# Input pieces and the order of the first tiles in a two-layer decoder kernel

## The chip, the cores and the metric

The kernel runs on one core of a Trainium2 chip. The time is the device time of one execution in microseconds (us), lower is better. Times of a kernel are compared as medians of several runs, and a profiler took one execution of the kernel before apart.

## The reference

A trunk of two layers runs over 512 prompt tokens and 8 decode tokens of width 1024, everything in float32. Each layer is two half-weighted feed-forward blocks around a mixer, each followed by a layer norm:

```
x <- LN(alpha*x + 0.5*SwiGLU_1(x))        D_MODEL = 1024, D_FF = 2816
x <- LN(alpha*x + mixer(x))               mixer: sparse attention (layer 0), pooling (layer 1)
x <- LN(alpha*x + 0.5*SwiGLU_2(x))
def _swiglu(x, w_i, w_o):
    h = jnp.einsum('btd,df->btf', x, w_i)
    gate, up = h[..., :D_FF], h[..., D_FF:]
    return jnp.einsum('btf,fd->btd', jax.nn.silu(gate) * up, w_o)
```

What matters here is the very first block: its input `x_prompt` (512 x 1024) and `x_sample` (8 x 1024), and its weights `ffn1_wi`.

## The kernel before

**Layout.** The activations live transposed in SBUF: `xf[p, d, t]` holds feature `128*d + p` of token `t`, for 8 tiles d of 128 features and 520 tokens. For precision each float32 matrix product is made of three products of a reduced float32 type: a tile is split into a high part (rounded) and a low part (the rest), for `x` as `xh` and `xl`, for the weights as `w_hi` and `w_lo`. TensorE (PE) multiplies hi*hi, hi*lo and lo*hi.

**Weights.** SyncE (SP) loads weight chunks of 1 MB into two buffers `w_raw` (L418: two DMAs of 512 KB for each chunk of `ffn1_wi`, in runs of 128 numbers, 512 bytes). ScalarE (ACT) makes `w_hi` in `split_hi` (L511), VectorE (DVE) makes `w_lo` in `split_lo` (L1221). SP may load chunk c once `s_lo` has reached c+1, which starts at 2: chunks 0 and 1 are loaded at once, chunk 2 after `split_lo(0)`.

**The start.** ACT issues eight DMAs (L733 to L741): the prompt's input as one DMA of 2 MB into `x_in` (rows of 4 KB), the decode input, the table of constants `const` (its first 128 columns are the identity that a transpose on PE needs), the page table twice, and three for the layer norms' parameters. All eight count on one semaphore, `s_in`. PE waits for all of them, transposes the parameters (L1169), then for each d the 4 token tiles of the prompt (L1175) and the 8 decode tokens (L1176) into PSUM; three pairs of banks take turns, so tile d waits for the copy of tile d-3 (`s_ev`). ACT runs `split_hi(0)` and `split_hi(1)` and only then copies `xf` to `xh` (L747). DVE runs `split_lo(0)` and `split_lo(1)`, then copies the parameters (L1698, L1700) and the tiles `xf` out of PSUM (L1704, L1705). GpSimd (POOL) waits for the eight DMAs, computes two columns of indices (L1842), starts a gather of 2 MB of cached keys (`fetch_half(0)`, L1749) and then computes `xl` (L1851).

**The first products.** In `two_chunks` PE multiplies the first half of the tokens with chunk 0, then with chunk 1, then the second half with both (192 matmuls, L797). It waits for `s_ev` at 8, for `s_lo` of the chunk, and for each tile's `xh`, and before the lo*hi part for each tile's `xl`. From there the loop over the chunks runs on, each engine in the fixed order of its program, to the end of the kernel. The gathered half of keys is written on by POOL at L1755, after the first two tiles of the hidden layer.

## Time and profile before

| | |
|---|---|
| median of 3 runs | 2185.98 us (2183.97 to 2189.35) |
| the profiled execution's own time | 2186.89 us |
| its span, first to last instruction | 2185.1 us |
| PE matmul busy | 2007.9 us (92%) |
| DVE, ACT, POOL busy | 856.9, 598.6, 513.3 us |
| HBM traffic | 81 GB/s over the span |

The profiled execution's own time is 1.8 us above its span and 0.9 us above the median. Every time below counts from the start of the span.

### The profile page before, as it was taken

Reading aid. Unit: us, or ns where it says so; the run is one execution under the profiler, and the core shown is the slowest. Engines: PE = TensorE matmul, PEld = TensorE weight load, DVE = VectorE, ACT = ScalarE, POOL = GpSimd, SP = SyncE. Lnnn points to the kernel's source line nnn. Section 1 sums busy time; section 2 is a strip of 40 time slices with the busy share of each in tenths; the row PEclk is TensorE's granted clock in tenths of the full one; section 3 lists DMA queues with packets and bytes.
Section 4 is the critical chain, followed back from the end, with each engine's and each line's share of the span. In section 5 each row is a group of like instructions: output and inputs, shape, how many; then the busy total and the mean of one; then the engine's idle time right before and its main releaser. Section 6 shows DMA issues by size and latency. Waiting matters only on the chain.

```text
span 2185.1 us, 36160 instructions
## 1 busy us (share of the span) xinstructions
PE 2007.9 (92%) x15485; PEld 1912.5 (88%) x15485; DVE 856.9 (39%) x1163; ACT 598.6 (27%) x837; POOL 513.3 (23%) x438
## 2 busy tenths in 40 slices
PE   5999999999897677999999999999998379999996
PEld 5999999976885457899999989999998379999996
DVE  2433322535836622543332254333224663333223
ACT  2221221422133242522122143212123452122123
POOL 2211121331400063511112132111121751111120
PEclk9999999988959868999999999999999689999998
DMA  5453322251100032233322322333221223332321
GB/s 169 135 173 96 89 83 99 69 145 39 42 1 1 5 94 78 58 96 96 96 83 83 105 78 77 96 96 93 82 101 33 59 60 96 96 88 85 101 74 40
DMA packets 258366, 179.55 MB, mean 82 GB/s; under 512 B 10806, under 2 KB 254782, under 8 KB 257757
## 3 DMA queue, kind: packets, MB, share of 16 engines
q1 hardware_dynamic: 250000, 154.90, 24.3%
q10 hardware_dynamic: 6165, 10.79, 1.8%
q0 software_dynamic: 2112, 12.59, 1.7%
q8 instruction: 67, 1.10, 0.2%
q14 instruction: 22, 0.18, 0.0%
HBM read 169.57 MB, written 8.08 MB: 81 GB/s over the span
## 4 chain that ended last, share of the span: by engine, by line
PE 81%; issue 6%; DVE 5%; ACT 3%; POOL 3%; DMA 1%; ACTq 0%; POOLq 0%; DVEq 0%
PE ps L797 69%; PE ps L896 3%; PE ps L840 2%; PE ps L901 1%; PE ps L998 1%; PE ps L914 1%; DVE xf L1247 1%; DVE xf L1253 1%; ACT w_hi L511 1%; DVE w_lo L1221 1%; PE ps L980 1%; POOL diag L1810 1%; PE ps L881 1%; POOL sum_sq L1734 1%; ACT xf L547 1%
## 5 line engine op out<-in xcount | busy, mean ns | idle before, releaser
L797 PE MATMUL ps<-xh,w_hi 128*128 128x260 f32 x3040 | 640.0, 286 | 39.5 <-ACT xh L542 17.8
L797 PE MATMUL ps<-xh,w_lo 128*128 128x260 f32 x3040 | 633.4, 284 | 0.0
L1221 DVE TENSOR_TENSOR w_lo<-w_raw,w_hi 128x2048 fp32r<-128x2048 f32 (+2 forms) x153 | 444.9, 2909 | 408.8 <-ACT w_hi L511 408.8
L797 PEld LDWEIGHTS ps<-xh,w_hi 128*128 128x128 f32 x3040 | 486.5, 191 | 45.1 <-issue 25.9
L797 PEld LDWEIGHTS ps<-xh,w_lo 128*128 128x128 f32 x3040 | 487.6, 191 | 0.2
L797 PE MATMUL ps<-xl,w_hi 128*128 128x260 f32 x3040 | 383.9, 283 | 1.3 <-POOL xl L1838 1.3
L797 PEld LDWEIGHTS ps<-xl,w_hi 128*128 128x128 f32 x3040 | 372.8, 189 | 1.7 <-POOL xl L1838 1.7
L511 ACT CAST w_hi<-w_raw 128x2048 fp32r<-128x2048 f32 (+2 forms) x153 | 281.9, 1843 | 283.2 <-PE ps L797 262.7
L797 PE MATMUL ps<-hh,w_hi 128*128 128x260 f32 x1408 | 292.9, 283 | 0.0
L797 PE MATMUL ps<-hh,w_lo 128*128 128x260 f32 x1408 | 291.4, 282 | 0.0
L1664 DVE TENSOR_TENSOR hid<-silu_g,ps 128x520 f32<-128x520 f32 x88 | 61.3, 696 | 548.5 <-ACT silu_g L710 514.7
L710 ACT ACTIVATE silu_g<-ps 128x520 f32<-128x520 f32 x88 | 53.3, 606 | 760.4 <-PE ps L797 760.4
L1742 POOL CAST hh<-hid 128x520 f32 (+1 forms) x88 | 54.6, 620 | 789.3 <-DVE hid L1664 789.3
L797 PEld LDWEIGHTS ps<-hh,w_lo 128*128 128x128 f32 x1408 | 224.1, 188 | 0.1
L797 PEld LDWEIGHTS ps<-hh,w_hi 128*128 128x128 f32 x1408 | 223.9, 188 | 0.1
L797 PE MATMUL ps<-hl,w_hi 128*128 128x260 f32 x1408 | 177.5, 282 | 0.0
L797 PEld LDWEIGHTS ps<-hl,w_hi 128*128 128x128 f32 x1408 | 172.1, 188 | 0.0
L1744 POOL TENSOR_TENSOR hl<-hid,hh 128x520 f32 (+1 forms) x88 | 115.7, 1314 | 14.3 <-POOL hh L1742 14.1
L1732 POOL TENSOR_TENSOR sum_z<-sum_z,xf 128x520 f32<-128x520 f32 x36 | 58.3, 1619 | 200.3 <-DVE xf L1229 196.5
L1870 POOL TENSOR_TENSOR xl<-xf,xh 128x260 fp32r<-128x260 f32 x64 | 70.4, 1118 | 101.1 <-ACT xf L547 100.7
L1734 POOL TENSOR_TENSOR sum_sq<-sum_sq,silu_g 128x520 f32<-128x520 f32 x36 | 68.5, 1903 | 0.0
L519 ACT ACTIVATE silu_g<-xf 128x520 f32<-128x520 f32 x36 | 22.7, 639 | 133.6 <-DVE xf L1229 120.1
(250 smaller groups left out, 1594.3 us busy)
## 6 DMA issues: line engine op xcount, KB each, us to landing
w_raw<-in_ffn_wi_dram SPq DMA_DIRECT2D x176, 512.0 KB
w_raw<-in_ffn_wo_dram SPq DMA_DIRECT2D x32, 1024.0 KB
w_raw<-in_ffn_wo_dram SPq DMA_DIRECT2D x16, 768.0 KB
w_raw<-in_attn_w_in_dram SPq DMA_DIRECT2D x8, 1024.0 KB
keys_scratch<-key_half POOLq DMA_DIRECT2D x2, 2048.0 KB, 7.9
w_raw<-in_attn_w_o_dram SPq DMA_DIRECT2D x4, 1024.0 KB
x_in<-in_x_prompt_dram ACTq DMA_DIRECT2D x1, 2048.0 KB
out_dram<-y_out ACTq DMA_DIRECT2D x4, 512.0 KB
```

What stands on the lines that cost most here:

```text
L511: nc.scalar.copy(w_hi[:, c % 2, 0:n], w_raw[:, c % 2, 0:n]).then_inc(s_hi, 1)
L710: nc.scalar.activation(halves(silu_g[:, j % 2, :]), ps[:, 4 * (j % 2):4 * (j % 2) + 2, 0:HT], ACT.Silu).then_inc(s_silu, 1)
L797: mm = nc.tensor.matmul(ps[0:mc, bank + 2 * m + h, 0:HT], w[:, k, m, 0:mc], x(k)[:, h * HT:(h + 1) * HT], start=first and k == 0 and w is ...
L840: mm = nc.tensor.matmul(ps[:, 2 * q + h, 0:HT], mean_ones, x[:, cols(h)], start=n == 0, stop=n == 2)
L896: nc.tensor.matmul(ps[0:mc, bank + h, 0:HT], w[:, k, m, 0:mc], xh[:, k, cols(h)], start=k == 0 and w is wh, stop=False)
L1221: nc.vector.tensor_tensor(w_lo[:, c % 2, 0:n], w_raw[:, c % 2, 0:n], w_hi[:, c % 2, 0:n].bitcast(F32), ALU.subtract).then_inc(s_lo, 1)
L1664: nc.vector.tensor_tensor(halves(hid[:, j % 2, :]), halves(silu_g[:, j % 2, :]), ps[:, b + 2:b + 4, 0:HT], ALU.mult).then_inc(s_free, 2)
L1732: nc.gpsimd.tensor_tensor(sum_z[:], sum_z[:], xf[:, d, :], ALU.add).then_inc(s_sum, 1)
L1734: nc.gpsimd.tensor_tensor(sum_sq[:], sum_sq[:], sq[:, d % 2, :], ALU.add).then_inc(s_sum, 1)
L1742: nc.gpsimd.tensor_copy(hh_ij, hid[:, j:j + 1, :]).then_inc(s_hh, 1)
L1744: nc.gpsimd.tensor_tensor(hl_ij, hid[:, j:j + 1, :], hh_ij.bitcast(F32), ALU.subtract).then_inc(s_hl, 1)
L1870: nc.gpsimd.tensor_tensor(xl[:, d, cols(h)], xf[:, d, cols(h)], xh[:, d, cols(h)].bitcast(F32), ALU.subtract).then_inc(s_x, 1)
```

## The change

The identity (128 columns of the table) and the decode input are loaded first, on a semaphore of their own. The prompt's input follows as four DMAs of 256 columns each (512 KB, rows of 1 KB), each with its own semaphore; the rest of the table and the five small DMAs come behind. PE starts a pair of tiles when its piece is there, uses four pairs of banks, and transposes the parameters last, just before the first product. ACT takes `xh` of tiles 0 to 2, then `split_hi(0)`, the other five `xh`, then `split_hi(1)`. DVE copies tiles 0 to 4, runs `split_lo(0)`, copies tiles 5 to 7, then the parameters, then runs `split_lo(1)`. POOL computes all `xl` ahead of the gather.

```diff
--- before.py
+++ after.py
@@ -261,6 +261,8 @@
 
 
         s_in = sem("s_in")
+        s_const = sem("s_const")
+        s_xin = [sem(f"s_xin{n}") for n in range(4)]
         s_raw = [sem("s_raw0"), sem("s_raw1")]
         s_hi = sem("s_hi")
         s_lo = sem("s_lo")
@@ -730,21 +732,24 @@
                 tail(ffn_w[name][2], st, 4 + 2 * (st.group + KF), nxt, False, not before_pool and nxt is not None,
                      POOL_ORDER if before_pool else range(KD), before_pool)
 
-            act.dma_start(x_in[:, 0:NQT, :], a["x_prompt"][0].rearrange("(i p) d -> p i d", p=P)).then_inc(s_in, 16)
-            act.dma_start(x_in[0:DEC, NQT, :], a["x_sample"].rearrange("b t d -> (b t) d")).then_inc(s_in, 16)
-            act.dma_start(const[:], a["c_table"]).then_inc(s_in, 16)
+            act.dma_start(const[:, 0:P], a["c_table"][:, 0:P]).then_inc(s_const, 16)
+            act.dma_start(x_in[0:DEC, NQT, :], a["x_sample"].rearrange("b t d -> (b t) d")).then_inc(s_const, 16)
+            for n in range(4):
+                act.dma_start(x_in[:, 0:NQT, 256 * n:256 * n + 256],
+                              a["x_prompt"][0, :, 256 * n:256 * n + 256].rearrange("(i p) d -> p i d", p=P)).then_inc(s_xin[n], 16)
+            act.dma_start(const[:, P:CONST_COLS], a["c_table"][:, P:CONST_COLS]).then_inc(s_in, 16)
             act.dma_start(table[:], a["page_table"].rearrange("(o b) n -> o (b n)", o=1).broadcast_to([P, DEC * N_PAGES]))\
                .then_inc(s_in, 16)
             act.dma_start(page_col[:], a["page_table"].rearrange("b (n o) -> (b n) o", o=1)).then_inc(s_in, 16)
             act.dma_start(lnp_rows[0:48, :], a["ln_g"].rearrange("l n (d p) -> (l n d) p", p=P)).then_inc(s_in, 16)
             act.dma_start(lnp_rows[48:96, :], a["ln_b"].rearrange("l n (d p) -> (l n d) p", p=P)).then_inc(s_in, 16)
             act.dma_start(lnp_rows[96:104, :], a["pool_scale"].rearrange("l (d p) -> (l d) p", p=P)).then_inc(s_in, 16)
-            split_hi(0)
-            split_hi(1)
-
             for d in range(KD):
+                if d == 3:
+                    split_hi(0)
                 act.wait_ge(s_ev, d + 1)
                 nc.scalar.activation(xh[:, d, :], xf[:, d, :], ACT.Copy).then_inc(s_xh, 1)
+            split_hi(1)
             for name in plan:
                 if name == "pr":
                     proj(name)
@@ -1165,17 +1170,20 @@
                 return mixer_out(name)
 
 
-            pe.wait_ge(s_in, 16 * 8)
-            nc.tensor.transpose(ps[:, 7, 0:104], lnp_rows[:], ident[0:104, 0:104]).then_inc(s_tr, 1)
+            pe.wait_ge(s_const, 32)
             for d in range(KD):
-                if d >= 3:
-                    pe.wait_ge(s_ev, d - 2)
-                b = 2 * (d % 3)
+                if d % 2 == 0:
+                    pe.wait_ge(s_xin[d // 2], 16)
+                if d >= 4:
+                    pe.wait_ge(s_ev, d - 3)
+                b = 2 * (d % 4)
                 for i in range(NQT):
                     nc.tensor.transpose(ps[:, b, i * P:(i + 1) * P], x_in[:, i, d * P:(d + 1) * P], ident)
                 nc.tensor.transpose(ps[:, b + 1, 0:DEC], x_in[0:DEC, NQT, d * P:(d + 1) * P],
                                     ident[0:DEC, 0:DEC]).then_inc(s_tr, 1)
+            pe.wait_ge(s_in, 16 * 6)
             pe.wait_ge(s_ev, KD)
+            nc.tensor.transpose(ps[:, 7, 0:104], lnp_rows[:], ident[0:104, 0:104]).then_inc(s_tr, 1)
             left = None
             for name in plan:
                 if name == "pr":
@@ -1692,17 +1700,18 @@
             nc.vector.memset(scratch[:, 0:1], 0.0).then_inc(s_lo, 2)
             nc.vector.memset(scratch[:, 1:2], 0.0).then_inc(s_used, 2)
             nc.vector.memset(scratch[:, 2:3], 0.0).then_inc(s_free, 4)
-            split_lo(0)
-            split_lo(1)
-            dve.wait_ge(s_tr, 1)
+            for d in range(KD):
+                dve.wait_ge(s_tr, d + 1)
+                b = 2 * (d % 4)
+                nc.vector.tensor_copy(xf[:, d, 0:SEQ], ps[:, b, :])
+                nc.vector.tensor_copy(xf[:, d, SEQ:TOK], ps[:, b + 1, 0:DEC]).then_inc(s_ev, 1)
+                if d == 4:
+                    split_lo(0)
+            dve.wait_ge(s_tr, KD + 1)
             n = step(nc.vector.tensor_copy(lnp[:], ps[:, 7, 0:104]))
             done(n)
             step(nc.vector.tensor_scalar(pool_gain[:], lnp[:, 96:104], 1.0 / ALPHA, None, ALU.mult))
-            for d in range(KD):
-                dve.wait_ge(s_tr, d + 2)
-                b = 2 * (d % 3)
-                nc.vector.tensor_copy(xf[:, d, 0:SEQ], ps[:, b, :])
-                nc.vector.tensor_copy(xf[:, d, SEQ:TOK], ps[:, b + 1, 0:DEC]).then_inc(s_ev, 1)
+            split_lo(1)
             for name in plan:
                 if name == "pr":
                     gone = proj(name)
@@ -1837,12 +1846,6 @@
                     pool.wait_ge(s_xh, st.x + d + 1)
                     nc.gpsimd.tensor_tensor(xl[:, d, :], diff[:, d, :], xh[:, d, :].bitcast(F32), ALU.subtract).then_inc(s_x, 1)
 
-            pool.wait_ge(s_in, 16 * 8)
-            for h in range(2):
-                x = nc.gpsimd.tensor_scalar(half_i[:, h:h + 1], page_col[:], 2.0, float(h), ALU.mult, ALU.add)
-            x.then_inc(s_zero, 1)
-            pool.wait_ge(s_zero, 1)
-            fetch_half(0)
             pool.wait_ge(s_free, 4)
             nc.gpsimd.memset(scratch[:, 0:1], 0.0).then_inc(s_hl, 2)
             nc.gpsimd.memset(scratch[:, 1:2], 0.0).then_inc(s_sum, 2)
@@ -1850,6 +1853,12 @@
                 pool.wait_ge(s_xh, d + 1)
                 nc.gpsimd.tensor_tensor(xl[:, d, :], xf[:, d, :], xh[:, d, :].bitcast(F32),
                                         ALU.subtract).then_inc(s_x, 1)
+            pool.wait_ge(s_in, 16 * 6)
+            for h in range(2):
+                x = nc.gpsimd.tensor_scalar(half_i[:, h:h + 1], page_col[:], 2.0, float(h), ALU.mult, ALU.add)
+            x.then_inc(s_zero, 1)
+            pool.wait_ge(s_zero, 1)
+            fetch_half(0)
             for name in plan:
                 st = plan[name]
                 if name == "pr":
```

## Rows read from the trace of the kernel before

**Rows 1.** The page, busy time by engine.
```profile
PE 2007.9 (92%) x15485; PEld 1912.5 (88%) x15485; DVE 856.9 (39%) x1163; ACT 598.6 (27%) x837; POOL 513.3 (23%) x438
```

**Rows 2.** The chain that ended last, 0 to 140: start, us, what.
```profile
32.23 24.60 PE ps L797 x192
56.83 0.08 issue
```

**Rows 3.** Timeline of PE: start, us, instruction [idle before <-releaser].
```profile
14.21 0.43 PE L1169 MATMUL ps<-const,lnp_rows 104*128 104x104 f32 x1 [14.21 <-DMA lnp_rows<-in_pool_scale_dram]
...
17.92 0.27 PE L1176 MATMUL ps<-const,x_in 8*128 8x8 f32 x1
25.07 1.12 PE L1175 MATMUL ps<-const,x_in 128*128 128x128 f32 x4 [6.88 <-DVE xf L1705]
...
26.32 1.11 PE L1175 MATMUL ps<-const,x_in 128*128 128x128 f32 x4
...
33.04 0.42 PE L797 MATMUL ps<-xh,w_lo 128*128 128x260 f32 x1
...
39.44 0.28 PE L797 MATMUL ps<-xh,w_hi 128*128 128x260 f32 x1
```

**Rows 4.** Timeline of ACT, 0 to 35.
```profile
4.58 0.35 ACTq L741 DMA_DIRECT2D lnp_rows<-in_pool_scale_dram  x1
...
16.29 1.90 ACT L511 CAST w_hi<-w_raw 128x2048 fp32r<-128x2048 f32 x1 [9.98 <-DMA w_raw<-in_ffn_wi_dram]
19.74 1.90 ACT L511 CAST w_hi<-w_raw 128x2048 fp32r<-128x2048 f32 x1 [1.56 <-DMA w_raw<-in_ffn_wi_dram]
...
32.21 0.64 ACT L747 ACTIVATE xh<-xf 128x520 fp32r<-128x520 f32 x1 [0.61 <-DVE xf L1705]
```

**Rows 5.** Timeline of DVE, 0 to 57.
```profile
18.22 2.29 DVE L1221 TENSOR_TENSOR w_lo<-w_raw,w_hi 128x2048 fp32r<-128x2048 f32 x1 [17.27 <-ACT w_hi L511]
...
23.88 0.26 DVE L1698 COPY lnp<-ps 128x104 f32<-128x104 f32 x1
...
24.26 0.68 DVE L1704 COPY xf<-ps 128x512 f32<-128x512 f32 x1
...
24.93 0.68 DVE L1704 COPY xf<-ps 128x512 f32<-128x512 f32 x1
...
32.02 0.15 DVE L1705 COPY xf<-ps 128x8 f32<-128x8 f32 x1
...
53.57 3.20 DVE L1221 TENSOR_TENSOR w_lo<-w_raw,w_hi 128x2048 fp32r<-128x2048 f32 x1 [1.04 <-ACT w_hi L511]
```

**Rows 6.** Timeline of POOL, 0 to 61.
```profile
15.56 1.20 POOL L1749 DMA_INDIRECT key_half<-in_cache_kidx_dram,half_i  x1 [0.96 <-POOL half_i L1842]
...
25.77 10.02 POOL L1851 TENSOR_TENSOR xl<-xf,xh 128x520 fp32r<-128x520 f32 x8 [8.86 <-ACT xh L747]
...
53.30 1.32 POOL L1744 TENSOR_TENSOR hl<-hid,hh 128x520 fp32r<-128x520 f32 x1
...
60.28 0.61 POOL L1755 DMA_DIRECT2D keys_scratch<-key_half  x1
```

**Rows 7.** Timeline of SP's queue, 3 to 4.
```profile
2.43 6.30 SPq L418 DMA_DIRECT2D w_raw<-in_ffn_wi_dram  x1
```

**Rows 8.** DMA queues, 3 to 4: packets, MB, share of 16 engines.
```profile
q10 hardware_dynamic: 58, 0.24, 95.2%
```

**Rows 9.** DMA queues, 6 to 7 (q10 is ACT's, q1 is SP's).
```profile
q10 hardware_dynamic: 90, 0.37, 90.1%
q1 hardware_dynamic: 91, 0.05, 15.4%
```

**Rows 10.** DMA queues, 11 to 12.
```profile
q10 hardware_dynamic: 79, 0.01, 27.9%
q1 hardware_dynamic: 83, 0.04, 16.8%
```

**Rows 11.** DMA queues, 14 to 15.
```profile
q1 hardware_dynamic: 631, 0.32, 117.8%
```

**Rows 12.** DMA queues, 4.9 to 5.3.
```profile
q1 hardware_dynamic: 5, 0.00, 2.1%
```

## The prediction

> **What bounds the kernel now.** I read the page first: PE is busy for 92% of the span [rows 1], so an edit at the start is worth only what it takes from the time before PE's unbroken run. The chain of waits says where that run starts. In its first 140 us it has nothing but PE's products: 192 matmuls from 32.23, then the loop of chunks with a gap of 0.08 us [rows 2]. So the change is worth 32.23 minus the new start of the first product, call it T, as long as nothing behind T comes later relative to it than now.
>
> Then I read the timelines of the engines, to see what makes T 32.23. PE starts at 14.21, when the last of ACT's eight DMAs has landed, transposes three tiles by 18.2, and then sits idle for 6.88 us, released by DVE's copy of tile 0 [rows 3]. DVE had started `split_lo(0)` at 18.22 and ran `split_lo(1)` before any copy; the copies begin at 24.26 [rows 5]. With the banks free again PE makes the last five tiles at 1.25 us each (25.07 to 26.32) [rows 3], DVE's last copy ends at 32.17 [rows 5] and the first product starts. What set the 18.22 is the weight chunk: ACT waited for chunk 0 until 16.29, took 1.90 us, and then had to wait for chunk 1 until 19.74 [rows 4]. The chain before, told backwards: last copy, five transposes, `split_lo(1)`, `split_hi(1)`, landing of chunk 1. The input had been in SBUF since before 14.21 and waited behind weights.
>
> **The change part by part.** The DMA queues come first, since they decide when chunk 0 lands; call that R0 (now 16.29).
>
> *Price of a packet.* From 14 to 15 only weight packets of 512 bytes ran: 631 packets for 117.8% of 16 engine-microseconds, 30 ns of engine time each [rows 11]. From 6 to 7 the input's 4 KB packets took 0.901 x 16 / 90 = 160 ns each, and the two queues moved packet for packet, 90 to 91 [rows 9]. The trace has no 1 KB packets; between the two sizes a straight line gives 30 + 130/7 = 49 ns, its bounds are 40 ns (a quarter of the 4 KB price) and 60 ns (two of 512 bytes). The input goes from 512 packets of 160 ns (82 us) to 2048 of 49 ns (100 us): 18 us over 16 engines is 1.1 us more, bounds 0 and 2.6. The identity's own 128 packets of 512 bytes add 0.2 us.
>
> *What moves behind.* The rest of the table is about 0.55 MB, the worth of 135 packets of 4 KB, 135 x 160 ns / 16 = 1.4 us. The small DMAs behind it run in a slow stretch, 79 and 83 packets in the whole of 11 to 12 against 631 in a good microsecond [rows 10, 11]; by such windows it lasted from 10.7 to 13, some 2.3 us with about 0.3 of useful weight traffic, so 2 us lost. Both lay in front of chunk 0's end before. Now 2184 packets (128, 8 and 2048) stand ahead of them on ACT's queue and chunk 0 has 2048 on SP's; if both ran packet for packet from the same time, chunk 0 would land first. But SP's packets began only near 4.9 [rows 12], about when ACT had issued its last DMA (4.93) [rows 4], though SP had issued from 1.09. ACT now issues twelve instead of eight, and SP's third issue stood for 6.30 us [rows 7], which tells me that a queue takes only so many packets ahead; ACT's may stand too. So R0 is bounded by two cases. All of the old work still in front: 16.29 + 1.1 + 0.2 = 17.6. The table's rest and the slow stretch entirely behind: 17.6 - 1.4 - 2.0 = 14.2. I take 16.0, about the middle: queue order puts them behind, the late start of SP's packets puts part of them in front.
>
> *From R0 to T.* Piece by piece the input lands well before: at the 0.21 MB/us that q10 gets next to weight packets (16 us / (49 + 30 ns) = 203 packets) plus the start alone, the last piece lands at 11 to 15. PE needs 1.25 us a tile and no longer waits for `split_lo`; tile 4 is copied by about 15.5, tile 7 is in PSUM by about 18. So DVE reaches `split_lo(0)` before its `w_hi` is there, and the chain is:
> - `split_hi(0)`: R0 + 1.90 + 0.03 [rows 4], 17.9. ACT has tiles 0 to 2 behind it by then.
> - `split_lo(0)`: 2.29 us with POOL idle [rows 5], 3.20 us in the case where POOL subtracts at the same time (53.57 beside 53.30) [rows 5, 6]. POOL will be at `xl` of tiles 3 and 4 then, so 3.2: 21.1. The bound below is 2.3.
> - three copies at 0.67 us (24.26 to 24.93) and the short one's end [rows 5]: 2.1 us, 23.2. They don't wait for PE.
> - new on the path: the transpose of the parameters now stands between the last copy and the first product, 0.43 us [rows 3], about 0.5 with its hand-over. T = 23.7.
>
> T = R0 + 7.7, where it was R0 + 15.9. The gain is 32.23 - 23.7 = 8.5 us. Removed are `split_lo(1)`, its wait for chunk 1 and five transposes with the copies' pace of 1.25; added are three quick copies, 0.9 us of slower subtraction and 0.5 us of transpose.
>
> *What is hidden, and by what.* `split_lo(1)`: ACT ends the last `xh` about 0.7 us after the last copy, as now (32.21 + 0.64) [rows 4], then 1.9 and 3.2 us: ready at T + 5.5. PE wants it when it goes to chunk 1, which is 7.2 us after the first product (39.44 against 32.23) [rows 2, 3]. The slack is 1.7 us; without it, each us late is a us lost. `xl`: 1.25 us a tile (10.02 / 8) [rows 6], the last near T + 2, wanted from T + 5. The gather: POOL now issues it near T + 2 = 26, with 1.20 us of POOL [rows 6]; its 2 MB then run between 28 and 34 instead of 18 to 23. It is next wanted at L1755, 28 us after the first product (60.28) [rows 6], so near 52. Chunk 2 is requested at 21 and wanted 19 us after T; it no longer meets the gather, chunk 3 may, with some 10 us to spare. The parameters' copy on DVE (0.26 us) [rows 5] and the five small DMAs are wanted at T only, and land by 18 even in the late case. I cost all of these at nothing.
>
> *The clock.* The first matmul rows take 0.42 us and later ones 0.28 [rows 3]: PE begins at the lower of its two levels (1.2 GHz) and changes about 3 us later, though it had transposed almost without a gap from 25.07. I expect the same after, since again a gap of some us stands before the first product, and cost it at nothing; it could be worth about 1.3 us either way (some 14 matmuls, 0.22 against 0.12 us apart).
> The Trainium skill (TensorE: Matmul & The Clock Gate, Part 1) says that the idle engine is throttled and that activity releases it. By that rule transposes might open the clock before the first product and add 1.3 us to the gain; the row shows that 6 us of them did not here.
>
> The time: 2186.89 - 8.5 = 2178.4 against the profiled execution. That one lies 0.9 above the median of the runs, so against the median I forecast 2185.98 - 8.5 = 2177.5 us, 0.39% less. A measurement of this kernel can tell about 0.3% from no change, or 6.6 us, so the forecast stands only 2 us beyond that edge.
>
> **The rivals.**
> - *The weights land late* (chance 0.19). The queues lose more than 1.3 us: 1 KB packets at 60 ns, a pause at the end of each DMA (in the slow stretch five DMAs cost some 2 us, 0.4 each; there are four more ahead of chunk 0 now), and SP's packets let in only after ACT's issues. That is 17.6 + 1.5 + 1.6 = 20.7 at worst; at 18 to 20.7 the gain is 6.5 to 3.8 us, about 2180.5. For it speaks SP's first packet at 4.9; against it, that engines working on one queue's packets are not lost to the other's, the sum stays.
>  The Trainium skill (DMA: Bandwidth & Descriptors, Measured and Anatomy of one DMA) speaks against the pieces: batch to 1 MiB or more, and a fixed cost near 2 us a DMA, fitted on another issue path. Taken one after another, four pieces would cost 6 us more than one whole, and an estimate by it leaves a gain of 2.5 us. In the trace the ends of successive DMAs overlap, so I don't take it.
> - *More is gained* (0.12). Chunk 0 lands at 14.2 and the subtraction takes 2.3: T = 21.0, gain 11.2; with an earlier clock change 12.5. Time 2174.
> - *The gain is given back behind T, or T hangs on something unseen* (0.03): for instance `split_lo(1)` misses its slack because chunk 1 lands after T + 2, or the gather holds up chunk 3. Gain 0 to 4, 2184. Chunk 1 would have to land beyond 25.7 against 19.74 now.
> - *Slower: the input's pieces go at the pace of the start* (0.03). From 3 to 4 the queue had the engines to itself and moved only 58 packets of 4 KB [rows 8]. If what limits it there is packets, not bytes, and lasts, 2184 packets of 1 KB at 58 a us need 38 us: the last piece lands at 41, and with two tiles, a copy and the parameters (3.8 us) T is 45, 13 us slower, 2199. It breaks even at a landing of 28.4, some 86 packets a us. Against it: by 6 the queues moved 181 packets a us, and 631 later [rows 9, 11].
>
> **How the numbers follow.** The likeliest case, a gain of 7 to 10.5 us, has the rest, 0.63. Its time is 2177.5 us. The range goes from the larger-gain case at 12 us (2174.0) to a gain of 4.5 us (2181.5), which takes in the bounds of R0 and of the subtraction, most of the late-weights case and the spread of the medians; the last two rivals stay outside, with the tails. Faster by over 0.3% is the likeliest case, the larger gain and a sliver of the late case, less the part of the likeliest case that a measurement's spread may push under the edge: 0.76. Within 0.3% is 0.20, slower 0.04.
>
> **What would show it right or wrong.** In the timeline after: PE's first transpose of tile 0 at 6 to 9, tile 7 by 18; ACT's first `w_hi` near 16.0; `split_lo(0)` at 3.2 us, ending near 21; copies 5 to 7 behind it back to back; L1169's row right before the first product, which starts near 23.7; no gap at PE's change to chunk 1 (7.2 us on); the gather near 26. The chain of waits should start with PE's products at T and be the old one from there. Wrong would be: `w_hi` after 18, a row of PE waiting for `w_lo` at T + 7, the first product released by something other than a DVE copy, or a later stage longer by more than a us.

## The result and the profile after

The changed kernel takes 2174.96 us (median of 5 runs, 2173.02 to 2175.64), the kernel before 2185.46 (5 runs, 2183.97 to 2189.35). The ratio is 0.9947, with a 95% interval of 0.9932 to 0.9962: faster by 0.4 to 0.7%. The profiled execution takes 2175.45 us with a span of 2173.6; against the profiled execution of before that is 11.4 us less, and 11.5 in the span.

The chain that ended last, first 21 us of the changed kernel (start, us, what). It begins with the input's first piece, not with a weight chunk:

```profile
1.80 7.01 DMA x_in<-in_x_prompt_dram
8.82 0.14 issue
8.96 1.08 PE ps L1181 x4
...
13.98 1.05 PE ps L1181 x4
15.03 0.22 PE ps L1182
15.24 0.02 issue
15.27 0.69 DVE xf L1706
15.96 0.07 DVE xf L1707
16.03 2.29 DVE w_lo L1229
...
19.66 0.60 DVE xf L1706
20.26 0.08 DVE xf L1707
20.34 0.14 issue
20.48 0.41 PE ps L1186
20.89 24.32 PE ps L802 x192
45.20 0.06 issue
45.27 94.78 PE ps L802 x790
```

The lines are those of the changed file: L1181 and L1182 are the transposes, L1706 and L1707 the copies, L1229 is `split_lo`, L513 `split_hi`, L1186 the parameters' transpose, L802 the products. From the piece's landing at 8.8 PE makes a tile each 1.25 us; the copy of tile 4 follows, then `split_lo(0)`, then three copies, then the parameters. The first product's own row starts at 20.61:

```profile
20.48 0.41 PE L1186 MATMUL ps<-const,lnp_rows 104*128 104x104 f32 x1 [1.51 <-DVE xf L1707]
20.61 0.56 PE L802 MATMUL ps<-xh,w_hi 128*128 128x260 f32 x1
```

It was 32.23 [rows 2], so T came 11.62 us earlier, and the span shrank by 11.5. Behind T nothing moved against it in these two executions. The first long run of products (2908 of them, the loop over the rest of the chunks) starts at 56.91 before and at 45.27 after, 24.7 us behind T in both. The second (the loop of the second feed-forward block) starts at 931.80 and at 920.18, 11.62 earlier.

ACT's timeline answers to [rows 4]:

```profile
9.27 0.35 ACTq L746 DMA_DIRECT2D lnp_rows<-in_pool_scale_dram  x1
...
13.57 0.64 ACT L751 ACTIVATE xh<-xf 128x520 fp32r<-128x520 f32 x1 [0.61 <-DVE xf L1707]
14.11 1.88 ACT L513 CAST w_hi<-w_raw 128x2048 fp32r<-128x2048 f32 x1
...
20.91 1.90 ACT L513 CAST w_hi<-w_raw 128x2048 fp32r<-128x2048 f32 x1
```

`split_hi(0)` has no idle time ahead of it: it runs at once behind `xh` of tile 2 at 14.11, so chunk 0 was there by then. When its packets ran is in the DMA queues (q1 is SP's, q10 is ACT's), from 4 to 5 (packets, MB, share of 16 engines):

```profile
q1 hardware_dynamic: 639, 0.32, 109.5%
```

and from 9 to 10:

```profile
q10 hardware_dynamic: 213, 0.21, 69.2%
q1 hardware_dynamic: 216, 0.11, 42.0%
```

SP's packets start at about 2.3 now and have the engines nearly to themselves until 5.3. Before, they started at 5.1: the five packets of [rows 12] all lie between 5.1 and 5.3. Windows of one us add up to 1950 weight packets by 7.0 and 2152 by 8.0, against 2048 in chunk 0, so by this count its data was through before 8. The input's 1 KB packets begin at 5.3 and soon share about 1:1 with chunk 1's; 213 packets of 1 KB in a good window is 52 ns of engine time each (0.692 x 16 / 213), and the windows from 6 to 14 give 48 to 53.

DVE and POOL, answering to [rows 5, 6] (timelines):

```profile
16.03 2.29 DVE L1229 TENSOR_TENSOR w_lo<-w_raw,w_hi 128x2048 fp32r<-128x2048 f32 x1
...
22.84 2.53 DVE L1229 TENSOR_TENSOR w_lo<-w_raw,w_hi 128x2048 fp32r<-128x2048 f32 x1 [0.85 <-ACT w_hi L513]
```

```profile
16.61 2.85 POOL L1854 TENSOR_TENSOR xl<-xf,xh 128x520 fp32r<-128x520 f32 x1 [1.04 <-ACT xh L751]
...
23.19 3.35 POOL L1854 TENSOR_TENSOR xl<-xf,xh 128x520 fp32r<-128x520 f32 x1
...
27.81 1.19 POOL L1758 DMA_INDIRECT key_half<-in_cache_kidx_dram,half_i  x1 [0.96 <-POOL half_i L1858]
```

`split_lo(0)` is not stretched by POOL. POOL's subtraction, started 0.58 us behind it, is: it ends at 19.46, 1.14 us behind DVE's end at 18.32, which is nearly the 1.28 us that it takes alone. The second case has both signs. DVE starts at 22.84, POOL's operation of the moment ends at 23.19, and DVE takes 0.24 us more than 2.29; POOL's next one starts at 23.19 and ends at 26.54, 1.17 us behind DVE.

### The profile page after: what moved, and what is told of

It is laid out like the page before. It is cut to its first block, busy times and chain, and to the rows that moved or that the text cites. A ratio compares the mean times of both kernels' runs of the same rounds, so it can differ in the third digit from the quotient of the medians.

```text
span 2173.6 us, 36167 instructions
## 1 busy us (share of the span) xinstructions
PE 2006.1 (92%) x15485; PEld 1911.4 (88%) x15485; DVE 857.8 (39%) x1163; ACT 597.7 (27%) x837; POOL 516.6 (24%) x438
## 4 chain that ended last, share of the span: by engine, by line
PE 80%; issue 7%; DVE 5%; POOL 3%; ACT 3%; DMA 1%; ACTq 0%; POOLq 0%; DVEq 0%
PE ps L802 70%; PE ps L901 3%; PE ps L845 2%; PE ps L906 1%; PE ps L1003 1%; PE ps L919 1%; DVE xf L1255 1%; DVE xf L1261 1%; DVE w_lo L1229 1%; ACT w_hi L513 1%; PE ps L985 1%; POOL diag L1819 1%; PE ps L886 1%; POOL sum_sq L1743 1%; ACT xf L549 1%
## 5 line engine op out<-in xcount | busy, mean ns | idle before, releaser
L802 PE MATMUL ps<-xh,w_hi 128*128 128x260 f32 x3040 | 640.7, 287 | 38.6 <-ACT xh L544 17.8
L802 PE MATMUL ps<-xh,w_lo 128*128 128x260 f32 x3040 | 633.6, 284 | 0.0
L1229 DVE TENSOR_TENSOR w_lo<-w_raw,w_hi 128x2048 fp32r<-128x2048 f32 (+2 forms) x153 | 445.2, 2911 | 390.7 <-ACT w_hi L513 390.7
L802 PEld LDWEIGHTS ps<-xh,w_hi 128*128 128x128 f32 x3040 | 486.7, 191 | 44.2 <-issue 25.8
L802 PEld LDWEIGHTS ps<-xh,w_lo 128*128 128x128 f32 x3040 | 487.8, 191 | 0.2
L802 PE MATMUL ps<-xl,w_hi 128*128 128x260 f32 x3040 | 383.8, 283 | 1.3 <-POOL xl L1847 1.3
L802 PEld LDWEIGHTS ps<-xl,w_hi 128*128 128x128 f32 x3040 | 372.7, 189 | 1.7 <-POOL xl L1847 1.5
L513 ACT CAST w_hi<-w_raw 128x2048 fp32r<-128x2048 f32 (+2 forms) x153 | 281.6, 1841 | 271.6 <-PE ps L802 262.8
L802 PE MATMUL ps<-hh,w_hi 128*128 128x260 f32 x1408 | 293.2, 283 | 0.0
L802 PE MATMUL ps<-hh,w_lo 128*128 128x260 f32 x1408 | 291.4, 282 | 0.0
L802 PEld LDWEIGHTS ps<-hh,w_lo 128*128 128x128 f32 x1408 | 224.2, 188 | 0.1
L802 PEld LDWEIGHTS ps<-hh,w_hi 128*128 128x128 f32 x1408 | 223.9, 188 | 0.1
L802 PE MATMUL ps<-hl,w_hi 128*128 128x260 f32 x1408 | 177.5, 282 | 0.0
L802 PEld LDWEIGHTS ps<-hl,w_hi 128*128 128x128 f32 x1408 | 172.1, 189 | 0.0
```

Of the source, the lines that this page charges most:

```text
L513: nc.scalar.copy(w_hi[:, c % 2, 0:n], w_raw[:, c % 2, 0:n]).then_inc(s_hi, 1)
L802: mm = nc.tensor.matmul(ps[0:mc, bank + 2 * m + h, 0:HT], w[:, k, m, 0:mc], x(k)[:, h * HT:(h + 1) * HT], start=first and k == 0 and w is ...
L1229: nc.vector.tensor_tensor(w_lo[:, c % 2, 0:n], w_raw[:, c % 2, 0:n], w_hi[:, c % 2, 0:n].bitcast(F32), ALU.subtract).then_inc(s_lo, 1)
```

## The experiments

The whole time is a blunt measure here. From the first long run of products to the second, the kernel before takes 874.89 us and the changed one 874.91, but the profiled executions of the experiments took 867.9 to 883.3, with the granted clock between 500 and 1000 us at 0.84 to 0.87. That stretch holds the attention part, which no edit here touches. So each experiment is read by T, the start of the first product's row, which the second run of the changed kernel repeated within 0.03 us. The ratios beside it compare the executions of each kernel (five for the first of the changed kernel, six to ten for the others) with the kernel before, run beside them.

T is not the whole of it. The third column is the start of the first long run of products, which is 24.6 to 25.8 us behind T in the kernels where nothing else is lost. The difference is PE's clock: the products' rows are at the low level until 3.0 us behind T in the changed kernel, and until 5.6 us in its second profiled execution, with the same instructions. The first long run came 1.2 us later there (46.47 against 45.27). So a gain in T of under about 1.2 us, against the changed kernel, can't be told behind T.

```profile
23.56 0.33 PE L802 MATMUL ps<-xh,w_lo 128*128 128x260 f32 x1
23.72 0.28 PE L802 MATMUL ps<-xh,w_hi 128*128 128x260 f32 x1
```

```profile
26.19 0.34 PE L802 MATMUL ps<-xh,w_lo 128*128 128x260 f32 x1
26.37 0.28 PE L802 MATMUL ps<-xh,w_hi 128*128 128x260 f32 x1
```

The first two rows are of the changed kernel, the other two of its second profiled execution (timelines of PE). The rows ahead of each pair have 0.42 us, those behind it 0.28.

| kernel | T | first long run | ratio to before, 95% |
|---|---|---|---|
| before | 32.23 | 56.91 | 1 |
| loads alone | 30.66 | 56.41 | 0.9996 (0.9973 to 1.0018) |
| engines' order alone | 25.65 | 51.15 | 0.9979 (0.9958 to 1.0001) |
| changed, one input DMA | 24.21 | 49.54 | 0.9977 (0.9954 to 1.0001) |
| changed | 20.61, again 20.64 | 45.27, again 46.47 | 0.9947 (0.9932 to 0.9962), again 0.9961 (0.9947 to 0.9975) |
| changed, gather first | 20.73 | 52.80 | one time, 2181.85 us |
| changed, each xl done twice | 21.21 | 55.83 | one time, 2178.79 us |
| changed, splits further ahead | 20.10, again 20.07 | 45.87, again 45.34 | 0.9936 (0.992 to 0.9953) |
| changed, a piece ahead of the identity | 19.76 | 44.36 | 0.9945 (0.9919 to 0.997) |
| input on SP | 21.29 | 46.17 | 0.9948 (0.9932 to 0.9964) |
| input on SP, small DMAs after tile 1 | 19.56 | 44.96 | 0.9954 (0.9937 to 0.9972) |
| input on SP, small DMAs after tile 3 | 19.88 | 45.00 | 0.9954 (0.994 to 0.9969) |

**The engines' order alone.** All of the change but its loads: the eight DMAs and the waits for all of them are those of before.

```diff
-            act.dma_start(const[:, 0:P], a["c_table"][:, 0:P]).then_inc(s_const, 16)
...
+            act.dma_start(x_in[:, 0:NQT, :], a["x_prompt"][0].rearrange("(i p) d -> p i d", p=P)).then_inc(s_in, 16)
+            act.dma_start(x_in[0:DEC, NQT, :], a["x_sample"].rearrange("b t d -> (b t) d")).then_inc(s_in, 16)
+            act.dma_start(const[:], a["c_table"]).then_inc(s_in, 16)
...
-            pe.wait_ge(s_const, 32)
+            pe.wait_ge(s_in, 16 * 8)
```

> The order of the engines' work as in the changed kernel, but the loads as before: one input DMA, then the decode input and the whole table, and PE and POOL wait for all eight. Theory (the order pays in the part from the input to the first product, the loads in when the input lands): the input is there at 14.2 as before, chunk 0 at 16.3. PE's tiles run at 1.25 us from 14.2, tile 2 is in xh by 18.9, so ACT starts w_hi near 19.4, w_lo ends near 23.7, three copies and the parameters' transpose follow: first product at 26.2, 6 us earlier than before, 2180. Rival (the loads are what pays, the order of the splits costs nothing since the weights' landing bounds it): first product at 30 or later, gain under 2.5 us.

T is 25.65, 6.6 us earlier than before, where 26.2 was expected. PE starts at 14.06, `split_hi(0)` at 19.25 behind `xh` of tile 2, with no wait for the chunk. The order alone moves the bound from the weights to PE's pace of 1.25 us a tile. The whole time can't be told from no change (0.9979, up to 1.0001), where 6.6 us would be 0.9970. Some of the gain in T was given back to the clock (the first long run came 5.8 us earlier), and the profiled execution had a long middle part (882.5 us); whether the others had it too isn't shown.

**The loads alone.** Identity first, four pieces, four bank pairs, parameters last, but both splits ahead of the first copy and the gather ahead of `xl`.

```diff
+            split_hi(0)
+            split_hi(1)
             for d in range(KD):
-                if d == 3:
-                    split_hi(0)
...
+            split_lo(0)
+            split_lo(1)
             for d in range(KD):
                 dve.wait_ge(s_tr, d + 1)
...
-                if d == 4:
-                    split_lo(0)
```

> The loads, the piece-wise start of PE, the four bank pairs and the late parameters as in the changed kernel, but ACT and DVE run both splits ahead of the first tile and POOL gathers first, as before. PE also waits for the parameters' copy before the first product, 0.4 us, as bank 7 needs it in this order. Theory: chunk 1 lands near 18 as its packets share with the input, w_lo(1) ends near 23, only then the copies start; PE has four tiles ready and makes four more at 1.25 us: first product at 29.5 to 30, gain 2 to 3 us, 2183. Rival (what pays is that the input comes in early): first product below 25, gain over 7.

T is 30.66, where 29.5 to 30 was expected: a gain of 1.6 us, of which PE's extra wait for the parameters' copy has already taken 0.4. Chunk 0's `w_hi` starts at 10.82, without a wait for the chunk, as soon as ACT has issued its DMAs and loaded its table, and then ACT waits for chunk 1:

```profile
10.82 1.90 ACT L513 CAST w_hi<-w_raw 128x2048 fp32r<-128x2048 f32 x1
18.87 1.90 ACT L513 CAST w_hi<-w_raw 128x2048 fp32r<-128x2048 f32 x1 [6.15 <-DMA w_raw<-in_ffn_wi_dram]
```

An early input is worth little while the copies stand behind a chunk that is late. Alone, the two halves of the change give 6.6 and 1.6 us; together they give 11.6.

**One input DMA.** The changed kernel with the identity and the decode input first and the input whole.

```diff
-            for n in range(4):
-                act.dma_start(x_in[:, 0:NQT, 256 * n:256 * n + 256],
...
+            act.dma_start(x_in[:, 0:NQT, :], a["x_prompt"][0].rearrange("(i p) d -> p i d", p=P)).then_inc(s_xin[0], 16)
...
-                if d % 2 == 0:
-                    pe.wait_ge(s_xin[d // 2], 16)
+                if d == 0:
+                    pe.wait_ge(s_xin[0], 16)
```

> The changed kernel with its input in one DMA of 2 MB behind the identity and the decode input; PE waits once. Tells the pieces from the order of issue. Theory (the queues are served in order of issue: chunk 0's packets go first because the identity lets SP issue ahead of the input): SP's packets again begin near 2.3 and chunk 0 is through by 8; the input has 4 KB packets, which gain on the weights' 1:1, and is whole at 11 to 12.5; PE starts 2.5 to 3.5 us later than the 8.96 of the changed kernel, the first product near 23.5, 2178. Rival (the pieces themselves let SP in early): SP's packets begin near 5 as before the change, the input lands by 10, w_hi waits for chunk 0 until 14 or later.

SP's packets begin at 2.3 here too; by windows the input's 4 KB packets begin only behind 5. T is 24.21, where 23.5 was expected, and PE starts at 12.55. So the pieces are worth 3.6 us. What let SP's weights in early was not the pieces but the order of issue. Before, and in the experiment with the old loads, the 2 MB DMA was issued at 0.77 and SP's first at 1.09, and SP's packets came at 5.1 and 4.9; here the 2 MB DMA is issued at 1.80. Nor was it the end of ACT's issues, which is at 5.6 here, 3.3 us behind SP's first packet.

**A piece ahead of the identity.**

```diff
+            act.dma_start(x_in[:, 0:NQT, 0:256], a["x_prompt"][0, :, 0:256].rearrange("(i p) d -> p i d", p=P)).then_inc(s_xin[0], 16)
             act.dma_start(const[:, 0:P], a["c_table"][:, 0:P]).then_inc(s_const, 16)
...
-            for n in range(4):
+            for n in range(1, 4):
```

> The changed kernel with the first input piece issued ahead of the identity and the decode input. Theory (order of issue): that piece's packets go out from 1.9 and it lands by 5; the identity, issued now behind SP's first weights DMA, lands near 6; PE starts near 6 instead of 8.96, and as each later piece lands in 2.2 us and a pair of tiles takes 2.5, PE stays the pace: first product 2 to 3 us earlier, near 18, 2172. Rival (the identity is held behind the whole of SP's first two DMAs, or the later pieces come as late as now): PE starts at 9 or later and nothing is gained.

T is 19.76, 0.85 us earlier; 2 to 3 were expected. PE starts at 7.11, when the decode input lands behind the identity, and makes two tiles; then it waits until 10.57 for the second piece, which like the changed kernel's pieces came behind SP's weights. SP's packets begin at 3.8, when the first piece's 512 have gone. The packets went out in the order of issue, as the theory says, but I had priced only the first piece and not the gap behind it.

**The splits further ahead.**

```diff
-                if d == 3:
+                if d == 1:
                     split_hi(0)
...
-                if d == 4:
+                if d == 1:
                     split_lo(0)
```

> The changed kernel with chunk 0's two splits further ahead: split_hi(0) ahead of xh of tile 1, split_lo(0) behind the copy of tile 1 instead of tile 4. Theory (chunk 0 is in SBUF by 8.5, and PE's pace of 1.25 us a tile from the landing of the first piece is the floor): the two splits are hidden behind PE's tiles, the last copy ends 0.8 us after PE's last tile (18.9), first product near 19.9, 0.7 us earlier than 20.6. Rival (chunk 0 lands late, near 14, as in the prediction): split_hi(0) holds up the xh tiles and split_lo(0) the copies, so that PE waits for its banks: first product after 21.

ACT takes `w_hi` at 11.46 with no wait: chunk 0 was in SBUF by then. With the 10.82 of the loads alone this is the plainest sign against the prediction's R0 of 16. T is 20.10, 0.5 us earlier. PE waits once for a bank (tile 6 at 16.49), so the pace of the tiles is nearly the floor. Timed:

> The kernel with chunk 0's splits behind tiles 0 and 1, timed this time. In its one look the first product came at 20.1 against 20.6 in the changed kernel; POOL's xl and DVE's split_lo(1) met less well (3.21 against 2.53 us), but with slack. Every theory: first product at 20.1; ratio to the kernel before 0.9945 within the spread.

The ratio is 0.9936 (0.992 to 0.9953), the best of all, though its interval and the changed kernel's overlap. The first long run starts at 45.87 and 45.34 in its two profiled executions, not earlier than the changed kernel's 45.27: a gain behind T isn't shown.

**The gather first.** The four lines with the wait for the small DMAs, the indices and `fetch_half(0)` go back ahead of POOL's `xl`.

```diff
+            pool.wait_ge(s_in, 16 * 6)
+            for h in range(2):
+                x = nc.gpsimd.tensor_scalar(half_i[:, h:h + 1], page_col[:], 2.0, float(h), ALU.mult, ALU.add)
...
+            fetch_half(0)
             pool.wait_ge(s_free, 4)
```

> The changed kernel with POOL's indices and gather ahead of its xl tiles again, as before the change. Theory (moving the gather behind xl is needed, since its wait for the small DMAs would hold up xl): the small DMAs land near 19, so POOL starts xl near 21.5 instead of 11.8 and ends the last tile near 32; PE wants xl 5.3 us behind its first product, at 26, and the tiles at that pace; xl of tile k is ready at 22.8 + 1.25 k, so PE waits little, under 3 us. The gather's 2 MB run against chunk 1 or 2. First product at 20.6 as in the changed kernel, then up to 3 us lost. Rival (the gather's place is free either way): nothing is lost behind the first product.

T is 20.73, but the first long run of products starts at 52.80 instead of 45.27: 7.5 us later, 7.4 of it behind T. POOL and DVE (timelines):

```profile
20.35 1.20 POOL L1758 DMA_INDIRECT key_half<-in_cache_kidx_dram,half_i  x1 [0.96 <-POOL half_i L1851]
...
21.64 10.05 POOL L1860 TENSOR_TENSOR xl<-xf,xh 128x520 fp32r<-128x520 f32 x8
```

```profile
21.33 10.38 DVE L1713 TENSOR_SCALAR pool_gain<-lnp 128x8 f32<-128x8 f32 x1
31.63 2.28 DVE L1229 TENSOR_TENSOR w_lo<-w_raw,w_hi 128x2048 fp32r<-128x2048 f32 x1
```

An operation of 8 elements a partition, which took 0.17 us in the kernel before and 0.77 in the changed one, stood on DVE for 10.38 us, until POOL had done all eight subtractions. `split_lo(1)` came behind it. PE waited 2.1 us for `xl` and then, at the end, 1.7 us for `w_lo` (waits of PE from 20 to 50); it went to chunk 1 at 33.97 instead of 27.81. Most of the rest of the 7.4 is that PE ran longer at its lower clock: its 62 hi*hi products from 20 to 50 average 331 ns, where a row at the low level has 0.42 us and one at the high level 0.28 [rows 3]. The rows are low until 5.8 us behind T, and again for 2.8 us from 33.97. The first of these stretches is nearly as long in the second profiled execution of the changed kernel, where nothing waits, and against that one the loss is 6.2 us and not 7.4. The loss that I expected (up to 3 us, by `xl` alone) was too small, since I left DVE out.

**Each xl twice.** A second subtraction into a spare tile ahead of each right one, on POOL.

```diff
+                if d > 0:
+                    pool.wait_ge(s_twice, d)
+                nc.gpsimd.tensor_tensor(sum_z[:], xf[:, d, :], xh[:, d, :].bitcast(F32), ALU.subtract).then_inc(s_twice, 1)
                 nc.gpsimd.tensor_tensor(xl[:, d, :], xf[:, d, :], xh[:, d, :].bitcast(F32),
```

> The changed kernel with each of POOL's eight xl subtractions done a second time into a spare tile ahead of the right one, so that POOL is busy without a gap from 11.8 on. Theory (a two-input operation on DVE and one on POOL do not run at once: the one that comes second waits until the other engine's has ended, and if POOL has its next one ready DVE goes on waiting): split_lo(0), ready at 16.03, lasts until POOL's run ends, some 6 to 9 us instead of 2.29, and the first product comes at 26 to 30. Rival (they share the bandwidth): split_lo(0) takes 2.3 to 4.6 us, first product at 21 to 23.

```profile
15.87 3.06 DVE L1230 TENSOR_TENSOR w_lo<-w_raw,w_hi 128x2048 fp32r<-128x2048 f32 x1
```

```profile
15.47 1.31 POOL L1858 TENSOR_TENSOR xl<-xf,xh 128x520 fp32r<-128x520 f32 x1
16.72 3.38 POOL L1857 TENSOR_TENSOR sum_z<-xf,xh 128x520 f32<-128x520 f32 x1
```

The theory's first half held, its second fell. DVE, started inside POOL's operation, waits for its end at 16.78 and ends 2.15 us later; POOL's next one waits for DVE's end at 18.93 and ends 1.17 us later. The two take turns, one whole operation at a time, rather than share. But DVE gets its turn after one operation, even with POOL busy without a gap: 0.8 us late, not 6 to 9. So the 10.38 us of the gather-first kernel is something more. The runs don't settle what: there POOL had just issued its gather (20.35), and all that its eight operations wait for had been reached. In the loads alone, where the gather is also issued at 20.32, the same DVE operation comes at 30.64, beside POOL's gapless subtractions, and takes 0.18 us. So a gather somewhere ahead does not do it by itself.

T is 21.21, inside the rival's 21 to 23, but the kernel loses 10.0 us behind T: the first long run starts at 55.83. PE waits three times for `xl`, 5.8 us in all, and from the last of these waits to 40.6 its rows are at the low level:

```profile
35.91 0.80 PE L803 MATMUL ps<-xl,w_hi 128*128 128x260 f32 x2 [1.97 <-POOL xl L1858]
```

So `xl` alone, when it is late enough, costs more than the gather did. The one time of 2178.79 us hides this, since its middle part was the shortest of all (867.9 us).

**The input on SP.** SP issues the pieces ahead of the weights, ACT the rest; `split_hi(0)` goes ahead of `xh` of tile 6, `split_lo(0)` behind the last copy.

```diff
+            for n in range(4):
+                sp.dma_start(x_in[:, 0:NQT, 256 * n:256 * n + 256],
+                             a["x_prompt"][0, :, 256 * n:256 * n + 256].rearrange("(i p) d -> p i d", p=P)).then_inc(s_xin[n], 16)
             for name in plan:
...
-                if d == 3:
+                if d == 6:
                     split_hi(0)
```

> SP issues the four input pieces ahead of its weights, ACT issues the identity, the decode input and the rest; split_hi(0) ahead of xh of tile 6, split_lo(0) behind the last copy. Theory (packets go out in order of issue, and the input is what PE's pace starts from): pieces land from about 4 to 10, PE starts by 5 and ends its tiles by 15; chunk 0 has to come by 13 to 14 behind the input; first product at 17.3 to 18.5, 2 to 3 us earlier than in the changed kernel, ratio 0.9935. Rival (the order of issue does not matter on one queue against two, or chunk 0 now is the late one): w_hi starts after 15.5 and the first product comes at 20.5 or later.

```profile
17.02 1.90 ACT L516 CAST w_hi<-w_raw 128x2048 fp32r<-128x2048 f32 x1 [1.07 <-DMA w_raw<-in_ffn_wi_dram]
```

Now chunk 0 is the late one, at 17.0, and T is 21.29. This is the case that I had predicted for the change itself: R0 + 1.90, `split_lo(0)` at 2.29, and the product. From 6 to 10 the rest of the table and the small DMAs ran between the pieces: from 9 to 10 only 96 packets of SP's and 92 of ACT's. Putting them later should free the weights. The changed kernel was timed again beside this one.

> The changed kernel itself again, for the comparison with the version above on one chip and for the spread of its time. Every theory: first product at 20.6 within 0.2; the time differs from run to run by what the stages behind it do, ratio 0.9945 to 0.996.

Its T is 20.64 and its ratio 0.9961 (0.9947 to 0.9975), a gain of 8.5 us where the first measurement gave 0.9947 (11.6); the kernel above has 0.9948 beside it. The intervals overlap.

**The small DMAs later.** The six DMAs behind `xh` of tile 1, or of tile 3.

```diff
             for d in range(KD):
+                if d == 2:
+                    act.dma_start(const[:, P:CONST_COLS], a["c_table"][:, P:CONST_COLS]).then_inc(s_in, 16)
...
```

> As the kernel with the input on SP, but ACT issues the rest of the table and the five small DMAs only behind xh of tile 1. Theory (in that kernel the small DMAs stood between the second and the third piece and held chunk 0 until 17.0; packets count in the order of issue): all four pieces land by 10, PE goes through its tiles without a gap and ends near 14.5; chunk 0 meets the small DMAs halfway and lands at 14.5 to 16; first product at 19 to 20, 1.5 to 2 us earlier than the 21.3 of that kernel. Rival (the loss there came from the pieces being on SP's queue): chunk 0 again near 17, first product at 21 or later.

> The same with the six DMAs issued behind xh of tile 3. Theory: chunk 0 is nearly through when they come, and lands at 13 to 14.5; ACT's issues cost it 3 us from 11.5 on, so xh of tile 4 and w_hi come at 14.7 to 15.3; w_lo ends near 19 and the first product starts at 19, unless the parameters, landing near 18, hold it up. Ratio 0.9935 to 0.995. Rival as above.

T is 19.56 and 19.88. In both PE goes through its eight tiles from 5.5 without waiting for a piece, as expected. In the first `w_hi` starts at 14.42 with no wait for the chunk, and `split_lo(0)`, started inside a subtraction of POOL, takes 3.17 us. In the second the parameters are late: they land at 19.7, 4.2 us after PE has done its tiles. So chunk 0 can come by 14.4 behind the whole input. The gain over the changed kernel is 1 us in T, 0.3 to 1.5 us at the first long run, and can't be told in the whole time.

## Why the prediction was right or wrong

**Right.** The bound (time ahead of PE's unbroken run, one to one: 11.62 us of T, 11.5 of span), the old chain told backwards, the direction and that it is clear of the measurement. 2174.96 lies in the range, near its lower end. The gain was undersized: 8.5 us of T forecast, 11.6 measured, 10.5 between the medians. The second measurement's ratio (0.9961) comes to 8.5 us, the forecast's gain, but that does not bear out its sum: T was 20.64 there too.

**The step that failed: R0, and with it the chain from R0 to T.** I took 16.0 for chunk 0's landing and hung all on it. By the count of packets it was through before 8, and ACT could take it without a wait at 10.82 (loads alone). It was not on the path at all. The late start of SP's packets [rows 12] I had tied to the end of ACT's issues at 4.93 [rows 4], and concluded that twelve issues would hold SP up longer. ACT's last issue is at 9.27 now and SP's packets begin at 2.3. What the runs show instead is that SP's packets came the later, the larger the DMA that ACT had issued just ahead of SP's first (1.09). With the 2 MB one at 0.77 they come at 5.1 (4.9 with the engines' order alone), with a piece of 512 KB at 3.8, with the identity (64 KB) at 2.3. And the input, issued at 1.80 behind SP's first, waits until 5.3, whole or in pieces (one-input kernel, changed kernel). What in the queues makes them wait isn't shown: with the input on SP the identity, issued on ACT 0.01 us behind SP's first piece, has packets from 2.4 on, in between the piece's. I had read the identity's move as 0.2 us of packets. As an order of issue it let the weights go ahead of the input.

**What was the bound instead.** The first piece's landing at 8.8 and PE's 1.25 us a tile, up to tile 4, whose copy ends at 16.03. `split_lo(0)` starts there instead of at 17.9: 1.9 of the 3.1 us that T came earlier than 23.7. That DVE would reach `split_lo(0)` ahead of its `w_hi` was wrong: `w_hi` ended at 15.99 and the copy of tile 4 at 16.03. Both are paced by PE's tiles, and the landing sets neither.

**Mis-sized terms.** `split_lo(0)`: 3.2 taken, 2.29 measured, 0.9 us. The 3.20 of 53.57 was a DVE operation that started 0.27 us inside POOL's [rows 5, 6] and waited for its end at 54.62; one that starts first is not stretched, and POOL pays. I used a duration where the trace had an order. The parameters' transpose: 0.5 taken; the last copy ends at 20.33 and the product's row starts at 20.61, so 0.3. The three copies took 2.0 from the end of `split_lo(0)` (18.32), where 2.1 was said. The packet of 1 KB was 48 to 53 ns where 49 was interpolated, inside its bounds. The start of `split_lo(0)` gives 1.9, its length 0.9, the transpose 0.2 and the copies 0.1: the 3.1 us between 23.7 and 20.6.

**Costed at nothing.** `split_lo(1)`: 22.84 + 2.53 = 25.4, wanted at 27.81; 2.4 us of slack. The gather is at 27.81 and nobody waits. But the move is needed: left ahead of `xl` the gather cost 7.4 us in this order (one execution), and the wait that ended last was for DVE's `w_lo`, not for `xl`. The clock: in the profiled execution the first products run at the lower level until about 23.6, 3 us, as before. That it costs nothing isn't so in each execution: 5.6 us in the second one, 1.2 us lost, which is nearly the 1.3 us that the prediction priced.

**The rivals.** Late weights: not here (they come at 17 only if the input and the small DMAs go ahead of them). More gained: nearest in size (11.6 against its 11.2), with the subtraction at its 2.3. But that `w_hi` started at 14.11, as it would with this rival's landing at 14.2, is chance: it started there behind `xh` of tile 2, with the chunk long landed. The fixed cost a DMA of the Trainium skill (DMA: Bandwidth & Descriptors, Anatomy of one DMA) doesn't show as 2 us for each piece: the pieces of the changed kernel follow at PE's pace and no tile after the first waits for one; in whole the four are worth 3.6 us against one DMA. The start's pace of 58 packets a us was no limit on packets: 639 a us went out from 4 to 5.

## What to carry to other kernels

At the start of this kernel, a DMA's place in the order of issue over both queues decided when its packets went, so a small one put first let the other queue's large one ahead. Read the first packet of each queue, not the issue. Before a landing is put on the path, look at what else the consumer stands behind: here three tiles at PE's pace would hide any landing up to 14. And where two engines' operations seem to slow each other, note which one started first before taking a duration from the row. And when a start time is used as the measure, follow it to the next fixed point of the program: two kernels here kept T within 0.6 us and lost 7.4 and 10.0 us right behind it.

## What the runs showed of the hardware

- DVE's and POOL's operations on SBUF here ran one at a time. The one that came second ended about its own length behind the other's end (1.14 to 1.17 us for POOL, 2.15 to 2.18 for DVE): POOL's 1.28 us became 2.85, 3.35 and 3.38, DVE's 2.29 became 2.53, 3.06 and 3.17. DVE's copies out of PSUM were not held (0.67 to 0.69 in all of these stretches).
- A DVE operation of 8 elements stood 10.38 us beside eight POOL subtractions without a gap, behind POOL's gather. Beside POOL's gapless pairs (each xl twice) the same operation took 0.80, and 0.18 beside its gapless subtractions 10 us behind a gather (loads alone). Why is open.
- The whole time depends on the stretch with the attention part, 867.9 to 883.3 us from the same instructions, with a granted clock of 0.84 to 0.87 from 500 to 1000: more than most edits of the start are worth.
- The first products ran at PE's low level for 2.7 to 5.8 us in the fourteen profiled executions, and for 3.0 and 5.6 us in the two of the changed kernel.
- PE's clock and transposes. In the changed kernel PE transposed without a gap from 8.96 to 18.9 and stayed at 1.25 us a tile. With the small DMAs after tile 1 it did so from 5.49, and the last tile came at 0.74 (14.02 to 14.76), where the others took 1.25:

```profile
12.78 0.27 PE L1183 MATMUL ps<-const,x_in 8*128 8x8 f32 x1
...
14.02 0.22 PE L1183 MATMUL ps<-const,x_in 8*128 8x8 f32 x1
...
14.76 0.22 PE L1183 MATMUL ps<-const,x_in 8*128 8x8 f32 x1
...
19.56 0.58 PE L803 MATMUL ps<-xh,w_hi 128*128 128x260 f32 x1 [2.59 <-DVE w_lo L1230]
```

  The clock had risen during transposes alone, and was low again at the first product after gaps of 1.67 and 2.59 us. The Trainium skill (TensorE: Matmul & The Clock Gate, Part 1) has activity release the clock; this run agrees. The changed kernel, and the one with the small DMAs after tile 3 (5.48 to 15.5), have as long a stretch of transposes and do not show it.
